# Moving twelve conditioning chunks out of the first projection loop, and three reorderings, in a hybrid decoder kernel

## The reference

```
mod = jnp.einsum('bd,de->be', c_act, w_ada[l]) + b_ada[l]
sh1, sc1, gt1, sh2, sc2, gt2 = [m[:, None, :] for m in jnp.split(mod, 6, axis=-1)]
h = x * (1.0 + sc1) + sh1
y, s_new, vn = token_mixer(h, s_all[l], ...)
x = layer_norm(ALPHA * x + gt1 * y, ln1_w[l], ln1_b[l])
h = x * (1.0 + sc2) + sh2
f_out = swiglu(h, ...) if l % 2 == 0 else moe_swiglu(h, ...)
x = layer_norm(ALPHA * x + gt2 * f_out, ln2_w[l], ln2_b[l])
```

## Time and profile before

| | |
|---|---|
| median of three runs | 1614.83 us (1614.65 to 1615.91) |
| the profiled execution | 1617.73 us, its span 1616.0 us |
| TensorE matmuls busy | 1516.9 us (94%), 8616 instructions |
| VectorE, ScalarE busy | 1174.0 us (73%), 907.8 us (56%) |
| DMA read | 407.79 MB, 257 GB/s over the span |
| w_lo of a chunk, w_hi of a chunk | 2286 ns x65, 1905 ns x65 |

### The profile page before, as it was taken

The page is one execution under the profiler, slowest core; times in us unless marked ns, Lnnn a source line. Parts: engine busy times, 40 slices in busy tenths (PEclk is TensorE's granted clock), DMA queues, the critical chain, the costliest instruction groups (busy, mean ns, idle before and its releaser), DMA issues.

```text
span 1616.0 us, 22378 instructions
## 1 busy us (share of the span) xinstructions
PE 1516.9 (94%) x8616; PEld 1277.5 (79%) x8616; DVE 1174.0 (73%) x1261; ACT 907.8 (56%) x845; POOL 62.0 (4%) x92
## 2 busy tenths in 40 slices
PE   5899998799999799988899999999999999999995
PEld 1667787699999699866788888888888888888874
DVE  2433557655566865665788988889888898888987
ACT  2444435343333365461676767677676776767762
POOL 2000010100000110002100000000000000000000
PEclk8899979899999999989999999999999999999998
DMA  9999935244444243132399999999999999999995
GB/s 322 327 353 335 349 98 158 83 158 150 140 154 148 88 151 127 53 111 66 135 354 350 358 333 358 336 347 349 335 364 329 344 348 333 363 339 366 350 362 176
DMA packets 217742, 416.06 MB, mean 257 GB/s; under 512 B 7923, under 2 KB 79773, under 8 KB 217638
## 3 DMA queue, kind: packets, MB, share of 16 engines
q1 hardware_dynamic: 214086, 402.31, 71.8%
q0 software_dynamic: 3552, 12.33, 2.6%
HBM read 407.79 MB, written 6.82 MB: 257 GB/s over the span
## 4 chain that ended last, share of the span: by engine, by line
PE 52%; DVE 5%; ACT 1%; issue 1%; DMA 1%; DVEq 0%; ACTq 0%
PE bank L665 14%; PE bank L667 14%; PE bank L666 14%; PE bank L1060 1%; PE bank L1098 1%; DVE w_lo L1582 1%; PE bank L668 1%; PE bank L670 1%; PE bank L669 1%; PE bank L765 1%; PE bank L1141 1%; PE bank L1142 0%; DMA raw_ring<-in_e_down_dram 0%; DVE w_lo L1573 0%; PE bank L1011 0%
## 5 line engine op out<-in xcount | busy, mean ns | idle before, releaser
L1582 DVE TENSOR_TENSOR w_lo<-raw_ring,w_hi 128x2048 fp32r<-128x2048 f32 x264 | 604.2, 2290 | 98.4 <-ACT w_hi L1311 97.7
L1311 ACT ACTIVATE w_hi<-raw_ring 128x2048 fp32r<-128x2048 f32 x264 | 506.7, 1919 | 231.8 <-PE bank L667 219.3
L665 PE MATMUL bank<-w_hi,xg_hi 128*128 128x512 f32 (+1 forms) x768 | 293.2, 382 | 3.0 <-DVE w_lo L1582 1.5
L667 PE MATMUL bank<-w_hi,xg_lo 128*128 128x512 f32 (+1 forms) x768 | 288.8, 376 | 0.0
L666 PE MATMUL bank<-w_lo,xg_hi 128*128 128x512 f32 (+1 forms) x768 | 288.8, 376 | 0.0
L668 PE MATMUL bank<-act_hi,w_hi 128*128 128x320 f32 x736 | 237.3, 322 | 29.2 <-DVE act_lo L1632 22.3
L669 PE MATMUL bank<-act_lo,w_hi 128*128 128x320 f32 x736 | 231.6, 315 | 0.0
L670 PE MATMUL bank<-act_hi,w_lo 128*128 128x320 f32 x736 | 231.1, 314 | 0.0
L1573 DVE TENSOR_TENSOR w_lo<-raw_ring,w_hi 128x2048 fp32r<-128x2048 f32 x65 | 148.5, 2286 | 82.4 <-ACT w_hi L1240 82.2
L668 PEld LDWEIGHTS bank<-act_hi,w_hi 128*128 128x128 f32 x736 | 142.3, 193 | 45.3 <-issue 38.9
L667 PEld LDWEIGHTS bank<-w_hi,xg_lo 128*128 128x128 f32 x768 | 144.3, 188 | 29.2
(11 more groups left out here) (329 smaller groups left out, 1916.4 us busy)
## 6 DMA issues: line engine op xcount, KB each, us to landing
raw_ring<-in_e_gate_dram SPq DMA_DIRECT2D x90, 1024.0 KB, 5.2
raw_ring<-in_e_up_dram SPq DMA_DIRECT2D x90, 1024.0 KB, 5.5
raw_ring<-in_e_down_dram SPq DMA_DIRECT2D x88, 1024.0 KB, 5.2
raw_ring<-in_w_ada_dram SPq DMA_DIRECT2D x24, 1024.0 KB, 6.8
raw_ring<-in_w_in_dram SPq DMA_DIRECT2D x24, 1024.0 KB, 7.5
st<-in_w_ada_dram SPq DMA_DIRECT2D x12, 1024.0 KB, 8.0
kdsp<-in_w_ada_dram SPq DMA_DIRECT2D x12, 1024.0 KB, 9.0
raw_ring<-in_w_ff_gate_dram SPq DMA_DIRECT2D x11, 1024.0 KB, 5.3
```

The lines of the kernel that those rows point to most:

```text
L665: pe.matmul(out, xh, wh, start=start, stop=False)
L667: return pe.matmul(out, xl, wh, start=False, stop=stop)
L1311: act.activation(w_hi[:, (NSPLIT + i) % SPL, :], raw[:, s, :], ACT.Copy).then_inc(hi_ready.sem, 1)
L1582: dve.tensor_tensor(w_lo[:, r, :], raw[:, s, :], w_hi[:, r, :].bitcast(F32), ALU.subtract).then_inc(lo_ready.sem, 1)
```

## The change

Only 36 of the 48 ada chunks stay in the start and the loop: w = 2 to 4 keep four, w = 5 to 10 have two. Of the other twelve, all of layer 1's conditioning, six are multiplied behind the last sums of layer 0's first layer norm, ahead of the dense stage, and six behind those of its second, ahead of layer 1's projection. They go through the common ring of four slots; their loads stand ahead of the dense stage's second gate chunk and of layer 1's third projection chunk. Their rows are copied to `accT` rather than `wide`. In the start, ada chunks 6 and 7 are loaded ahead of the first two weight chunks, and those two are split while the input is modulated. The last level goes between the first and second gMLP tile, with VectorE's differences ahead of it. On VectorE, the first residual column goes ahead of the first renewal, and two low parts and a modulation go later; on ScalarE the state scaling of heads 1 to 3 is put between the output projection's squares.

```diff
@@ -97,38 +97,47 @@
     GROUPS = {(0, 1): 1, (0, 3): 1, (0, 5): 1, (1, 0): 1}
     for w in range(2, NWIN - 1):
-        if WIN_ORDER[w] // 2 in (1, 4):
-            GROUPS.update({(w, 0): 1, (w, 1): 1, (w, 2): 2})
+        tok = WIN_ORDER[w] // 2 in (1, 4)
+        if w < 5:
+            GROUPS.update({(w, 0): 1, (w, 1): 1, (w, 2): 2} if tok else {(w, 0): 2, (w, 1): 2})
         else:
-            GROUPS.update({(w, 0): 2, (w, 1): 2})
-    PER = 4
+            GROUPS.update({(w, 0): 1, (w, 2 if tok else 1): 1})
+    LATE = 6
+    NEARLY = NALL - 2 * LATE
     group_ada, n = {}, ADA_A
     for key, cnt_ in GROUPS.items():
         group_ada[key] = list(range(n, n + cnt_))
         n += cnt_
...
-    order = [("ada", i) for i in range(6)] + [("w", 0), ("w", 1)] + [("ada", i) for i in (6, 7, 8)]
+    assert n == NEARLY
+    order = [("ada", i) for i in range(8)] + [("w", 0), ("w", 1), ("ada", 8)]
     order += [("w", 2), ("ada", 9), ("w", 3), ("ada", 10), ("ada", 11)]
-    for w in range(NWIN - 4):
-        a = PER * (w + 3)
-        order += [("ada", a), ("ada", a + 1), ("w", w + 4), ("ada", a + 2), ("ada", a + 3)]
-    a = PER * (NWIN - 4 + 3)
-    order += [("ada", i) for i in range(a, NALL)] + [("w", i) for i in range(NWIN, NSPLIT)]
+    a = ADA_A + 4
+    for w in range(NWIN - 2):
+        n = sum(c for (v, _), c in GROUPS.items() if v == w + 2)
+        order += [("ada", i) for i in range(a, a + n // 2)] + ([("w", w + 4)] if w + 4 < NWIN else [])
+        order += [("ada", i) for i in range(a + n // 2, a + n)]
+        a += n
+    late = {split_index["gate", 0, 1]: NEARLY, split_index["win", 1, WIN_ORDER[2]]: NEARLY + LATE}
+    for i in range(NWIN, NSPLIT):
+        order += [("ada", late[i] + j) for j in range(LATE)] if i in late else []
+        order += [("w", i)]
...
+    loads, landed, times, holds, ring = [], {}, [0] * (RAW + 2), [None] * (RAW + 2), 0
     for key in order:
-        s = weight_slot(key[1]) if key[0] == "w" else 2 + key[1] % 4
+        if key[1] < (NWIN if key[0] == "w" else NEARLY):
+            s = key[1] % 2 if key[0] == "w" else 2 + key[1] % 4
+        else:
+            s, ring = ring % RAW, ring + 1
         loads.append((key, s, holds[s]))
         times[s] += 1
         holds[s] = key
@@ -637,7 +646,13 @@
         def ada_bank(p):
+            if p >= NEARLY // 2:
+                return (5, 6, 7)[p % 3]
             return (6, 5 if ADA_A // 2 <= p < FREE_7 else 7)[p % 2]
+        def ada_wide(p):
+            return wide[:] if p < NEARLY // 2 else accT[:].rearrange("p k t -> p (k t)")[:, 0:2 * CW]
         def scatter_bank(e, m):
...
+                    pe.wait_ge(var_ready.sem, var_ready.at(0, 0))
                 b = bank[ada_bank(p)]
@@ -835,7 +856,6 @@
                         last.then_inc(ws_T.sem, 1)
                     if w > NWIN - NL:
                         level(l, w - (NWIN - NL) - 1)
-                level(l, NL - 1)
                 pe.wait_ge(vn_ready.sem, vn_ready.at(l))
                 pe.wait_ge(ws_read.sem, ws_read.at(l, 1))
@@ -849,6 +869,8 @@
                         last = pe.matmul(b[:, h * n:(h + 1) * n], vtok[0:n, t, h * P:(h + 1) * P],
                                          wsT[:, h, :] if t < 2 else wsS[:, h, :], start=False, stop=(h == H - 1))
                     last.then_inc(mx_mm.sem, 1)
+                    if t == 0:
+                        level(l, NL - 1)
                 pe.wait_ge(qk_ready.sem, qk_ready.at(l))
                 for t, t0, n in VTILES:
...
                 if l == 0:
+                    for i in range(NEARLY, NEARLY + LATE):
+                        ada(i)
...
                                 last.then_inc(done.sem, 1)
+                    ada_turn()
                     for kind, c in FFN_ORDER[2:]:
                         wh, wl = split_chunk((kind, 0, c))
...
                         sums(l, 1, m)
+                    for i in range(NEARLY + LATE, NALL):
+                        ada(i)
...
                         act.activation(act_hi[:, ks, :], out[:, ks, :], ACT.Copy).then_inc(h_hi.sem, 1)
+                        if (l, i, a) == (0, 0, 0):
+                            make_hi(1)
                     elif a >= 2:
...
             act.activation(lt[:, 2:4, :], lt[:, 0:2, :], ACT.Exp).then_inc(lt_exp.sem, 1)
-            make_hi(1)
             ada_rows(6)
             ada_rows(7)
+            make_hi(0)
             evs = [0]
             for l in range(DEPTH):
                 modulated(l, 0, hmix)
+                if l:
+                    ada_rows(NALL - 2)
+                    ada_rows(NALL - 1)
                 base = split_index[("win", l, WIN_ORDER[0])]
@@ -1402,23 +1442,24 @@
                 root(1)
                 mixed(0)
                 mixed(1)
-                make_hi(base + 2)
                 mixed(2)
-                for h in range(H):
-                    act.wait_ge(qs_mm.sem, qs_mm.at(l, h))
-                    for b in range(NB):
-                        c0 = TP + (b + 1) * DS - 1
-                        last = act.activation(states[h][:, b, :], states[h][:, b, :], ACT.Copy, scale=fe[:, h, c0:c0 + 1])
-                    last.then_inc(st_kept.sem, 1)
+                keep_state(0)
                 for j in range(KD):
                     make_hi(base + j // 2 + 2)
                     if j >= 2:
                         squares(l, 0, j - 2)
+                        if j in (2, 4, 6):
+                            keep_state(j // 2)
                 squares(l, 0, KD - 2)
                 squares(l, 0, KD - 1)
                 deviation(l, 0)
+                if l == 0:
+                    for i in range(NEARLY, NEARLY + 4):
+                        ada_rows(i)
                 modulated(l, 1, hf)
                 if l == 0:
+                    for i in range(NEARLY + 4, NEARLY + LATE):
+                        ada_rows(i)
                     at = {key: split_index[(key[0], 0, key[1])] for key in FFN_ORDER}
                     make_hi(at[("gate", 1)])
                     for c in range(NFC):
@@ -1437,6 +1478,8 @@
                     for m in range(KD):
                         squares(l, 1, m)
                     deviation(l, 1)
+                    for i in range(NEARLY + LATE, NALL - 2):
+                        ada_rows(i)
             act.wait_ge(rt_mm.sem, 1)
...
                     if w == 1 and l:
+                        for p in range((NEARLY + LATE) // 2, NALL // 2):
+                            ada_sums(p)
                         modulation(l, 1)
@@ -1829,20 +1875,19 @@
                         last = dve.tensor_tensor(vtok[0:n, t, :], vtok[0:n, t, :], lnb[0:n, :], ALU.add)
                         if w == 11:
                             last.then_inc(vn_ready.sem, 1)
-                take(NL - 2)
-                take(NL - 1)
-                dve.wait_ge(P_read.sem, P_read.at(l, NL - 1))
+                dve.wait_ge(Z_ready.sem, Z_ready.at(l, NL - 2))
                 for h in range(H):
                     for s0, s1, j in ((0, TP, P), (TP, T, DS)):
                         B4 = bc[:, h, s0:s1].rearrange("p (b j) -> p b j", j=j)
                         last = dve.tensor_tensor(D_[:, h, s0:s1].rearrange("p (b j) -> p b j", j=j),
                                                  B4[:, :, j - 1:j].to_broadcast([P, (s1 - s0) // j, j]), B4, ALU.subtract)
                 last.then_inc(D_ready.sem, 1)
+                take(NL - 2)
                 dve.wait_ge(eb_ready.sem, eb_ready.at(l))
-                dve.tensor_tensor(q[:, :, 0:TP], q[:, :, 0:TP], fe[:, :, 0:TP], ALU.mult)
                 dve.wait_ge(D_ready.sem, D_ready.at(l, NL - 1))
                 dve.memset(qs, 0.0).then_inc(qs_zero.sem, 1)
+                take(NL - 1)
+                dve.tensor_tensor(q[:, :, 0:TP], q[:, :, 0:TP], fe[:, :, 0:TP], ALU.mult)
                 dve.wait_ge(qs_zero.sem, l + 1)
                 dve.tensor_tensor(bc[:].rearrange("p h (b x) -> p h b x", x=40)[:, :, :, 0:DS],
                                   q[:, :, TP:T].rearrange("p h (b s) -> p h b s", s=DS),
@@ -1928,25 +1973,27 @@
                 scaled(2)
                 low_b(0)
                 low_b(1)
-                make_lo(base + 1)
                 gate_b(2)
                 low_b(2)
-                renew(0, bank[3:5])
-                expand(2)
-                if l == 0:
-                    modulation(1, 0)
+                make_lo(base + 1)
                 gt = 2 * KD
                 for m in range(KD):
-                    make_lo(min(base + m // 2 + 2, base + NWO + 1 if l == 0 else base + NWO - 1))
+                    if m:
+                        make_lo(min(base + m // 2 + 2, base + NWO + 1 if l == 0 else base + NWO - 1))
                     if m in (3, 5, 7):
                         renew(m // 2, bank[3:5])
                         if m == 3:
                             expand(3)
                     dve.wait_ge(wo_mm.sem, wo_mm.at(l, m))
```

(9 more changed lines are left out.)

31 lines of the change are left out of this document (20 added, 11 removed).

## The result

The changed kernel takes **1575.2 us** (median of four executions, 1572.3 to 1578.5) where the kernel before takes 1614.7 beside it: a ratio of 0.9756, with a 95% interval of 0.9744 to 0.9768, a gain of 39.5 us or 2.4%. The forecast was 1577 and a gain of 37.9. So the two traces are 45.4 us apart, not 39.5; terms that are read from this pair of traces come out some us too large in sum.

The account below looks back on a forecast made before the run. Loads were taken to bound the start and TensorE the projection loop, with short waits elsewhere. Terms 2.7 + 16.4 + 8 + 11.5 - 0.7 = 37.9 us took the median from 1614.83 to 1576.9, said as 1577, range 1568 to 1588.

Parts of the forecast that it names:

- Loop, 16.4: Layer 0's projection loop: column tiles w = 5 to 10 lose a chunk pair of 2.74 us each, 16.4 us gained.
- Start, 2.7: Before layer 0's first matmul: modulation done beneath the weight loads, first matmul at 43.9 instead of 46.70, 2.7 us gained.
- the wait of which I was afraid: Loop behind the start: a 2.5 us wait, put down to a late weight chunk, that could undo the start's gain.
- Last level, 8: Last level in both layers: first mixing tile fills the wait, k ready 4.1 us sooner; 8 us gained, bounds 3.5 and 9.
- First residual, 11.5: Output projection, both layers: waits of 1.8 and 3.1 us go; 6.5 plus 5, 11.5 us gained, bounds 7.4 and 13.
- The first centring: Behind renewal, expansion and a low part, wanted by the sums after column 2; about 1.2 us of wait stays.
- State scaling, nothing: ScalarE in the output projection: spreading the scaling costs nothing, since ScalarE waits for TensorE; at most 2.4 us.
- Holes, -0.7: Two layer norm holes, six chunks each: 0.8 us gained in the first, 1.5 lost in the second; bounds -5 and +4.
- Rival 2: Clock stays up with idle gone at five places, holes at +4; 45 us gained, 1570 us; chance 0.10.
- Rival 1: VectorE takes over in the loop and the start's gain is lost; 28 us gained, 1586 us; chance 0.16.
- Rival 3: Holes become longer, later dense stage chunks wait for loads, 74 us over 31 chunks; 1651 us; chance 0.03.
- Rival 4: Loads, not matmuls, bound the loop, so 38 us go there rather than 16; 1555 us; chance 0.02.

Follow-up runs that it names:

- e2: Changed kernel with the last level ahead of the mixing again and VectorE's copy, subtractions and zeroing in the old order; 1584.6 us, ratio 0.9801.
- e7: Changed kernel with the sixth chunk of each hole moved behind the first 12 matmuls of the following block; 1577.9 us, ratio 0.9774.
- e9: Changed kernel with the state scaling in one piece ahead of the output projection, residual still ahead of the renewal; 1594.4 us, ratio 0.9858.
- e1: Changed kernel with its twelve late conditioning chunks back in the projection loop, both holes empty; 1589.5 us, ratio 0.9833.
- e4: Changed kernel with the old start, conditioning loads 7 and 8 behind the first two weight chunks; 1579.1 us, ratio 0.9776.
- e10: Changed kernel with VectorE's conditioning sum ahead of the four scans in column tile w = 3 of layer 0; 1570.3 us, ratio 0.9712.
- e3: Changed kernel with the first residual behind renewal, expansion, modulation and a weight low part again, state scaling in one piece; 1587.2 us, ratio 0.9825.
- e6: Changed kernel with its twelve late chunks left out altogether, both holes idle for 8.7 us; 1575.1 us, ratio 0.9748.
- e5: Changed kernel run again unchanged, as the base on another chip; 1576.2 us, ratio 0.9757.
- e12: Changed kernel with the conditioning sum ahead of the scans and empty matmuls (36, 8, 9 and 28) in TensorE's idle time; 1568.1 us, ratio 0.9699.
- e8: Changed kernel with four late chunks in each hole and the other four back in the loop; 1579.9 us, ratio 0.9779.
- e11: Changed kernel with empty matmuls in TensorE's idle time, 60 ahead of layer 0 and 8, 10 and 44 in the three holes; 1574.2 us, ratio 0.9737.

## Why the prediction was right

*Loop, 16.4.* Right. The tile w = 6 takes 13.03 us, the forecast's 13.0; the stretch gave 17.9, of which six times 2.73 are 16.4. The other 1.5 is within what this stretch varies by without an edit to it (149.4 to 151.7 in eight traces: after, e2 to e7 and e9), and e1 gave 12 to 14 in the whole time. "All on the path" holds, and VectorE did not take over: no level wait shows in layer 0.

*Start, 2.7.* Right by the trace (46.70 to 43.97) and by e4 (2.9 at the first matmul, 3.9 in the median). It lasts, since the wait of which I was afraid did not grow (2.1 us against the 2.5 of the earlier trace rows). I had put that wait down to a late weight chunk alone. It is the wait for a conditioning sum that VectorE makes behind that chunk's low part and behind four scans (2.96 us); e10 shows that going ahead of the scans is enough to end it.

*Last level, 8.* Right in mechanism; 7 to 9.4 by e2's times, 8.9 by its stretches, and 10.1 between the traces before and after, over my upper bound of 9. The level runs at the full clock, as assumed; k's transposes start 4.85 and 4.7 us sooner rather than 4.1. Three small errors add up to that 0.75: the level starts 0.24 us later and not 0.5, it gains 1.6 (4.16 - 2.56) where I wrote 1.5, and VectorE's way from the copy to k is 3.5 us shorter, not 3.1 (from 6.50 to 3.02). e2's layer 0 shows that the 1.6 of clock in it is not certain.

*First residual, 11.5.* Right in mechanism; 11 to 12 by e3's times, 14.3 by the traces. Layer 1, put at 5, gave 6.7 in the trace after and 4.9 to 5.1 against e1, e2 and e5. Layer 0, put at 6.5, gave 7.6. There I had expected idle time and some of the half clock to go; the half clock ahead of the column's wait was hidden, as e3 shows, but its 1.5 us came back all the same once VectorE's way to the column was short. The first centring, put at 1.2 us, waits 0.4.

*State scaling, nothing.* The value was right and the reason too narrow. My reason, "ScalarE waits for TensorE in each of these columns", says only that the spread pieces find room; e9 shows that the spreading is also what makes the moved high part harmless, worth 16 to 18 us. I priced the edit that was made, and not what it protects.

*Holes, -0.7.* Right, as far as can be told: -1.2 by the stretches, -1.1 by e6, both within chance of zero. The lengths were 2 and 3 us more, as worked out from the slots and loads. The clock gave 2.7 and 1.3 back in the first trace, 1.1 and 1.0 in e5. That the second is so small is the trace before: its second block lost only 1.35 us behind an idle time of 8.71, where the same empty hole in e1 and e6 cost 2.8, and 1.5 more in the next 48 matmuls. Rival 2's +4 did not come: the loads were late, as the length of both holes shows.

*The rivals.* Rival 1 (1586) fell with the 13.03 and the kept start. Rival 2 (1570) fell for this kernel, whose short waits still drop the clock in some executions; e12 stands at 1568, with the waits filled and the sum moved, of which the sum alone (e10, 1570.3) is the larger part. Rival 3 (1651): the stretch of hole one and dense stage is 255.2 against 255.6, with no new wait for a load in it. Rival 4 (1555) fell with the loop's 17.9.

The sum was off by 1.6 us in the medians, which is less than its terms are known to; some of that closeness is luck. Terms read from the two traces add up to 45.4, because one profiled execution was slower and the other faster than its median.

## What to carry to other kernels

Where a program has two like tiles, one with the extra work and one without, take a term from their difference: it gave the largest one here, 13.02 forecast and 13.03 measured for the tile. Price a moved instruction also by what it stands behind on its own engine: an edit that costs nothing can be what keeps another from costing 18 us, and undoing it alone is the test. Where TensorE is the bound, add to an idle time what the half clock behind it may cost: here mostly 2.5 to 2.8 us in the 96 matmuls behind 3.6 to 8.7 us of idleness, and nothing or some 1.5 us behind 2 us. Count that only where TensorE sets the time; where it would wait for VectorE anyway, the slow stretch is hidden. Fill the idle time with useful work; empty matmuls that end just inside the wait kept the clock up as well, though by the times alone their worth is not shown.

## What was not expected of the hardware

Empty holes of 8.7 us (e1, e6) and waits of 4.46 and 3.57 us (e8) cost the block behind them nearly the same, 16.8 to 17.1 us for matmuls that take 14.35. The exception is the second hole of the trace before, with 15.7 behind 8.71 us. Waits of some 2 us drop the clock in some traces and not in others, and among these it isn't the length that decides. Behind the wait for the sum in column tile w = 3, the stretch from the first chunk to the end of the next 24 split matmuls took 7.2 us in five traces (waits of 2.05 to 2.48: before, after, e1, e5, e6) and 5.7 in four others (1.95 to 2.80: e2, e4, e8, e9); with waits of 1.44 and less (e3, e7, e11) it always took 5.7. What decides between the two isn't shown by any run here.

The changed kernel has several such waits, and its executions spread over 6 to 7 us, where the kernel before on the same two chips stayed within 2. Why e12 still spreads over 4 us, and why the kernel before did so over 7.5 us on the chips of e9 and e12 and not on the others, stays open.
